# A hybrid decoder step on one core: the second output gate computed between key units, sample products in quarters, the third modulation round spread out

## The chip, the cores and the metric

The kernel runs on one core of one Trainium2 chip, as a single launch. The metric is the device time in microseconds, the median of several runs. Inputs and outputs lie in HBM; everything between them is held in the core's on-chip memory (SBUF, 128 partitions) and in eight accumulator banks (`ps`, PSUM). The engines are TensorE (PE), VectorE (DVE), ScalarE (ACT), GpSimd (POOL) and SyncE (SP), each with its own instruction queue that is worked off in order; they are kept in step by semaphores (`sem(...)`), written out by hand.

## What is computed

One layer for 256 prompt tokens and 8 sample sequences of 4 tokens (288 tokens in all, `T`), model width 1024, all in float32. From the reference, cut:

```python
mod = jnp.dot(jax.nn.silu(c), w_ada) + b_ada             # 6 x 1024 per sequence
sh1, sc1, gt1, sh2, sc2, gt2 = split(mod, 6)
h = rmsnorm(x, g_pre1) * (1.0 + sc1) + sh1
hq, hf, hi, hg, aq, ak, av, ua, ub = split(h @ w_in)     # 4 x 512, 3 x 512, 2 x 1024
# branch a: gated linear recurrence over hq, hf, hi, from state_hgrn for the samples, normed, times silu(hg)
# branch b: attention; samples against 2048 cached keys and values each (16 pages of 128 tokens,
#           found through page_table), of which the best 3 of 8 blocks of 256 and the own tokens count
merged = sigmoid(ua) * (o_a @ w_proj_a) + sigmoid(ub) * (o_b @ w_proj_b)
x = x + gt1 * rmsnorm(merged @ w_out, g_post1)
h = rmsnorm(x, g_pre2) * (1.0 + sc2) + sh2
g_, u_ = split(h @ w_gu)                                 # 2 x 2816
x = x + gt2 * rmsnorm((silu(g_) * u_) @ w_down, g_post2)
```

Outputs are x, the new recurrent states, and the new keys and values.

## The kernel before

**Dense products.** Activations lie transposed, features on partitions, the 288 tokens along the free dimension. A weight tile has 512 input features times 512 columns (1 MB). Since the product is to be as exact as float32, weights and activations are split in a high part and a remainder (`w_hi`, `w_lo`, `h_hi`, `h_lo`), and each product is three matmuls (`three`, lines 1399 to 1401). ScalarE copies a half tile into the high part (L540, and `hi_late`, L555), VectorE subtracts to get the remainder (L897, `lo_late` L906), then TensorE does 24 matmuls of 128x288 for the half tile, 48 for the tile. Tiles 0 to 13 of w_in (`dense_in`) fill `w_hi` and `w_lo`, which have two buffers. Tiles 14 to 21, which give the two output gates `ua` and `ub`, use `wl_hi` and `wl_lo`, with one buffer.

**The ring.** All weights and cached pages go through `ring`, four slots of 1 MB. The list `RING` fixes the order; SyncE issues the loads in this order, and load n waits in `slot_free` until the content of slot n - 4 has been used: a modulation tile (`w_ada`) by its TensorE group (`ada_used`), a w_in tile by the subtraction of its second half (`lo_split`), a key unit by its transpose, a value unit by its matmuls. A key or value unit is four pages of 256 KB.

**Stages.** First the norms and the first modulation round (8 tiles of w_ada); then w_in tiles 0 to 13, with the second round (tiles 8 to 15) in pairs ahead of tiles 0, 2, 3 and 4 and the third (16 to 23) in pairs ahead of tiles 10 to 13. Rotation of q and k, the gate products of the samples (`queries` on GpSimd, L450), the samples' own scores (L1527) and the start of the recurrence lie between them.

Then the *key stage*: 32 key units (`cached_keys`). VectorE transposes a unit into `KT` (two buffers, L1060), TensorE does 32 small matmuls (L1546), and after each four units `restrip` (L1553) rearranges the scores. The list `between` puts other work behind single units: transposes of the recurrence (L1583), and behind units 5, 7, ... 19 the eight `gram` products (L1598) in two sets of banks. Each level of the recurrence goes from GpSimd (`diff`, L464 and L465) to ScalarE (`level_exp`, L647), back to GpSimd (`scale_level`, L475), to TensorE (`gram`), and to VectorE (`keep`, L1084).

Then tiles 14 to 17, while VectorE chooses blocks and ScalarE takes the exponentials; the first value unit (L1565) comes behind tile 17. In the *value stage* (32 units, `values`) the list `after` puts work behind single units: tiles 18 to 21 behind units 1, 3, 5 and 7, the recurrence's output (`hgrn_out`, L1620), the samples' reads of their states (`hgrn_sample_out`, L1627 and L1630: per head 8 matmuls of four columns, with a 128x128 weight load each), `sample_states` (L1639), and from unit 13 the eight heads of the prompt's attention (`prompt_step`: scores, then a mask and a maximum on VectorE from L1223, an exponential on ScalarE L745, normalisation on VectorE, transposes and value products). The four `o_normed` (L1205) and four `sample_state` (L1177, L1184) stand between the first heads on VectorE.

Then the projections, the merge and `w_out`; the *x1 stage* (norm, residual, second norm): channels 0 to 5 of the residual on VectorE (L1312, L1314), channels 6 and 7 on GpSimd (L496, L498), which also does the three operations on the sample tokens (L503 to L508) and all eight `h_lo` of `h_lower(1)` (L436). The feed-forward part follows, and at its end sums over the tokens' features (`token_sums`, L1808) in two groups, in banks 7 and 2, added on VectorE (L1383).

Of the kernel before, what the change touches and what calls it, by code (L numbers as in the profile page):

```python
# [16 lines left out]
F32 = mybir.dt.float32  # L17
# [3 lines left out]
ALU = mybir.AluOpType  # L21
# [35 lines left out]
def constants():  # L57
# [42 lines left out]
    c["seq"] = (p[:, None] // TS == np.arange(NSEQ)[None, :]).astype(float)  # L100
# [15 lines left out]
def build(nc, inp, out):  # L116
# [55 lines left out]
    wl_lo = sb("wl_lo", [P, BK, BC], F32R, "split_area", BK * BC * 4)  # L172
    proj = sb("proj", [P, PT_, T], F32, "proj_area")
# [78 lines left out]
    GROUPS = [4, 5, 6, 1, 0, 2, 3, 7, 8, 9, 10]  # L252
    NF = 7
    NKU = NVU = 4 * NSEQ
    SAMP = slice(TP, T)
    U_BANK = ((4, 7), (5, 0), (6, 1))
    ROOT2 = slice(384, 387)
    ADA_BANK = (4, 6)
    X1_DVE = 6
# [24 lines left out]
    def w_src(name, row, col, rows=BK * P, width=BC):  # L284

        return inp[name][0, bass.ds(row, rows), bass.ds(col, width)].rearrange("(k p) n -> p k n", p=P)

# [18 lines left out]
    with block:  # L306

        @block.sync
        def _(sp):
# [36 lines left out]
            for j in range(4):  # L346
                pages = page_numbers(SPE, 4 * j, 4)
                slot_free(NA + j)
                load_pages(sp, "cache_k", pages, (NA + j) % NSLOT)
            with sp.Fori(1, NSEQ) as b:  # L350
                for j in range(4):
                    pages = page_numbers(SPE, b * NPG + 4 * j, 4)
# [1523 lines left out]
```

## Time and profile before

| | |
|---|---|
| median of 3 runs | 765.85 us (760.8 to 769.72) |
| the profiled execution | 767.38 us, its span 765.5 us |
| mean granted TensorE clock | 0.912 of full speed |
| busy: TensorE, VectorE, ScalarE, GpSimd | 657.4, 413.2, 273.8, 77.2 us |
| HBM traffic | 168.93 MB, mean 221 GB/s |
| DMA busy, tenths in 40 slices of the span | 8895952978999978896565998540464546445201 |
| chain that ended last | PE 66%, DVE 12%, DMA 9%, POOL 4%, SyncE's queue 4%, issue 3%, ACT 2% |

Times inside the kernel are microseconds from the start of the span. The busy time of an engine is the time in which it executes; TensorE's matmuls overlap, so its busy time counts pipelined work. A dense matmul has a mean of 302 ns in the records, but one starts every 131 ns. "Idle before" says what ended an engine's wait. The granted clock is the share of full speed that the chip gave TensorE in a stretch: 1.0 is 2.4 GHz, 0.5 is 1.2 GHz. The DMA share is the mean busy share of the core's 16 DMA engines.

### The profile page before, as it was taken

The numbers are of one execution on the slowest core, as the hardware profiler recorded it, in microseconds if no ns is written. First come the engines' busy times: TensorE is split into PE (matmuls) and PEld (weight loads), VectorE is DVE, ScalarE is ACT, GpSimd is POOL, SyncE is SP. The second block draws the span as 40 slices with busy tenths as digits, with TensorE's granted clock in tenths as the row PEclk, the third lists the DMA queues.
The fourth block names the chain that finished last, engine by engine and source line by source line (L and its number), as shares of the span: only waits on it lengthen the run. The fifth ranks groups of instructions, "written<-read, shape, count | busy, mean of one in ns | idle before, by whom it ended". The sixth has DMA issues, their size and how long they took to land.

```text
span 765.5 us, 13144 instructions
## 1 busy us (share of the span) xinstructions
PE 657.4 (86%) x5251; PEld 552.0 (72%) x5251; DVE 413.2 (54%) x493; ACT 273.8 (36%) x390; POOL 77.2 (10%) x86
## 2 busy tenths in 40 slices
PE   4759999986867769889967759985999999999996
PEld 1237999774655559768423329984999999999996
DVE  0641479357999979320387325767635353543522
ACT  1232435253221136223312223353645454532421
POOL 2040005101364000000000000004200000000001
PEclk9859999997999699997668959998999999999987
DMA  8895952978999978896565998540464546445201
GB/s 334 318 349 209 357 186 87 353 252 290 351 332 307 336 287 230 290 324 203 188 210 157 325 343 274 184 148 0 124 188 153 172 143 190 150 151 182 87 1 62
DMA packets 96305, 168.93 MB, mean 221 GB/s; under 512 B 6449, under 2 KB 37865, under 8 KB 93058
## 3 DMA queue, kind: packets, MB, share of 16 engines
q1 hardware_dynamic: 90386, 162.85, 62.7%
q10 hardware_dynamic: 5152, 3.08, 1.4%
q0 software_dynamic: 720, 2.32, 0.8%
q8 instruction: 35, 0.57, 0.3%
q14 instruction: 12, 0.10, 0.0%
HBM read 163.51 MB, written 4.72 MB: 220 GB/s over the span
## 4 chain that ended last, share of the span: by engine, by line
PE 66%; DVE 12%; DMA 9%; POOL 4%; SPq 4%; issue 3%; ACT 2%; POOLq 0%; DVEq 0%; ACTq 0%
PE ps L1399 17%; PE ps L1401 16%; PE ps L1400 16%; DMA ring<-w_in 6%; DVE KT L1060 4%; SPq L302 2%; DMA ring<-w_ada 2%; PE ps L1565 2%; PE ps L1410 2%; POOL hx L475 2%; PE ps L1598 2%; PE ps L1630 2%; PE ps L1546 2%; PE ps L1762 1%; DVE wl_lo L906 1%
## 5 line engine op out<-in xcount | busy, mean ns | idle before, releaser
L897 DVE TENSOR_TENSOR w_lo<-ring,w_hi 128x1024 fp32r<-128x1024 f32 (+1 forms) x112 | 133.4, 1218 | 124.9 <-ACT w_hi L540 124.8
L1399 PE MATMUL ps<-h_hi,w_hi 128*128 128x288 f32 x576 | 174.1, 302 | 14.4 <-POOL h_lo L436 9.5
L1400 PE MATMUL ps<-h_lo,w_hi 128*128 128x288 f32 x576 | 172.0, 299 | 0.0
L1401 PE MATMUL ps<-h_hi,w_lo 128*128 128x288 f32 x576 | 171.3, 297 | 0.0
L540 ACT ACTIVATE w_hi<-ring 128x1024 fp32r<-128x1024 f32 (+1 forms) x112 | 113.8, 1040 | 153.7 <-PE ps L1401 87.1
L1399 PEld LDWEIGHTS ps<-h_hi,w_hi 128*128 128x128 f32 x576 | 109.9, 191 | 22.5 <-issue 13.1
L1401 PEld LDWEIGHTS ps<-h_hi,w_lo 128*128 128x128 f32 x576 | 110.4, 192 | 0.0
L1400 PEld LDWEIGHTS ps<-h_lo,w_hi 128*128 128x128 f32 x576 | 110.3, 191 | 0.1
L1060 DVE STREAM_TRANSPOSE KT<-ring 128x2048 f32<-128x2048 f32 x32 | 72.3, 2286 | 9.1 <-PE ps L1546 5.7
L1546 PE MATMUL ps<-KT,Wk 128*32 128x128 f32 x1024 | 39.4, 303 | 21.4 <-DVE KT L1060 21.4
L1546 PEld LDWEIGHTS ps<-KT,Wk 128*32 128x32 f32 x1024 | 29.8, 120 | 32.9 <-DVE KT L1060 23.3
L1399 PE MATMUL ps<-f_hi,w_hi 128*128 128x288 f32 x176 | 53.5, 304 | 0.0
L1400 PE MATMUL ps<-f_lo,w_hi 128*128 128x288 f32 x176 | 53.1, 302 | 0.0
L1401 PE MATMUL ps<-f_hi,w_lo 128*128 128x288 f32 x176 | 52.9, 301 | 0.0
L1399 PE MATMUL ps<-h_hi,wl_hi 128*128 128x288 f32 x128 | 38.7, 303 | 9.2 <-DVE wl_lo L906 9.1
L1565 PE MATMUL ps<-ring,Pt 128*32 128x512 f32 x256 | 39.1, 709 | 6.8 <-DMA ring<-cache_v 6.8
L1410 PE MATMUL ps<-ring,cs 128*32 128x512 f32 x192 | 29.3, 723 | 14.5 <-DMA ring<-w_ada 14.5
L1400 PE MATMUL ps<-h_lo,wl_hi 128*128 128x288 f32 x128 | 37.8, 295 | 0.0
L1401 PE MATMUL ps<-h_hi,wl_lo 128*128 128x288 f32 x128 | 37.6, 294 | 0.0
L1401 PEld LDWEIGHTS ps<-f_hi,w_lo 128*128 128x128 f32 x176 | 34.3, 195 | 0.0
L1399 PEld LDWEIGHTS ps<-h_hi,wl_hi 128*128 128x128 f32 x128 | 24.0, 187 | 14.2 <-DVE wl_lo L906 14.2
L1399 PEld LDWEIGHTS ps<-f_hi,w_hi 128*128 128x128 f32 x176 | 34.2, 194 | 0.0
(314 smaller groups left out, 1004.7 us busy)
## 6 DMA issues: line engine op xcount, KB each, us to landing
ring<-cache_k SPq DMA_DIRECT2D x128, 256.0 KB, 4.0
ring<-cache_v SPq DMA_DIRECT2D x128, 256.0 KB, 3.6
ring<-w_ada SPq DMA_DIRECT2D x24, 1024.0 KB, 7.5
ring<-w_in SPq DMA_DIRECT2D x22, 1024.0 KB, 7.8
ring<-w_gu SPq DMA_DIRECT2D x44, 512.0 KB, 4.7
ring<-w_down SPq DMA_DIRECT2D x10, 1024.0 KB, 5.0
ring<-w_out SPq DMA_DIRECT2D x4, 1024.0 KB, 5.4
S<-state_hgrn SPq DMA_DIRECT2D x4, 512.0 KB, 7.3
```

Of the source, the lines that this page charges most:

```text
L302: queue.dma_start(ring[:, s, q * 512:(q + 1) * 512], pools[pool][0, bass.ds(pg, 1), :, :].rearrange("o p n -> p (o n)"))\
L475: ins = pool.tensor_tensor(xv, xv, sv, ALU.mult)
L540: act.activation(w_hi[:, par, k, :], slot4(s)[:, k, :], ACT.Copy).then_inc(sem("hi_split"), 1)
L897: dve.tensor_tensor(w_lo[:, par, k, :], slot4(s)[:, k, :], w_hi[:, par, k, :].bitcast(F32), ALU.subtract).then_inc(sem("lo_split"), 1)
L1060: dve.transpose(KT[:, u % 2, :, :], ring[:, s, :].rearrange("p (g n) -> p g n", n=512)).then_inc(sem("key_slots"), 1)
L1399: pe.matmul(dst, h, x_hi, start=first, stop=False)
L1400: pe.matmul(dst, h, x_lo, start=False, stop=False)
L1401: return pe.matmul(dst, l, x_hi, start=False, stop=last)
L1410: ins = pe.matmul(ps[32 * i:32 * i + 32, ADA_BANK[g % 2], :], cs[:, k, :], ring[:, n % NSLOT, i * BC:(i + 1) * BC], start=k == 0, stop=k = ...
L1546: ins = pe.matmul(ps[32 * a:32 * a + 32, b % 2, j * P:(j + 1) * P], Wk[:, b, m // 2, 2 * a + m % 2, :], KT[:, u % 2, :, c * 32:(c + 1) * 3 ...
L1565: ins = pe.matmul(ps[32 * q:32 * q + 32, g, :], Pt[:, 4 * g + q, i, :], ring[:, n % NSLOT, q * 512:(q + 1) * 512], start=i == 0, stop=False)
L1598: ins = pe.matmul(ps[:, 2 + 2 * (gi % 2) + tt, h * P:(h + 1) * P], left[:, h, tt * P:(tt + 1) * P], right[:, h, tt * P:(tt + 1) * P], star ...
```

## The change

**Input stage.** The third modulation round is no longer loaded in pairs ahead of tiles 10 to 13: one tile comes after each of the tiles 7 to 10, two after 11 and two after 12 (`ADA_AFTER`), in ring and TensorE order alike, and it has a bank of its own. The samples' spread and own scores move together between tiles 8 and 9, the four small operations on `lbt` move ahead on VectorE, and the logarithm and the exponential of the recurrence ahead of `evac_in` on ScalarE. The first key transposes wait only for the dense tiles that used their part of the memory.

**Key stage.** The four tiles of the second output gate `ub` are cut otherwise: `WK`, 1024 input features by 256 columns, each in the ring behind key units 5, 11, 17 and 23. They are worked in eight groups of 24 matmuls (`dense_k`) behind key units 6, 9, ... 27, with new buffers `wk_hi` and `wk_lo` for half a tile, a copy on ScalarE (`hi_k`), the subtraction on GpSimd (`lo_k`) and evacuation by `evac_k`. GpSimd's eight `queries` are spread among its levels. All `gram` results use banks 2 and 3, and `keep` comes one unit earlier.

**Value stage.** Only the four tiles of `ua` (`WL`, 18 to 21) stay behind the keys: three ahead of the values, the last in two halves behind units 1 and 2. The samples' state reads become eight products of 512 columns, four heads side by side in quarters of the array (`sample_reads`), masked on VectorE into `xm`, and added up by eight transposing matmuls. The prompt steps stand behind every second unit from 10 on.

**x1 and the end.** All eight channels of x1 go to VectorE, GpSimd keeps one of three sample operations, the first two `h_lo` go to VectorE. The last token sums are one group in bank 7, read straight by ScalarE.

```diff
-    ADA_BANK = (4, 6)
-    X1_DVE = 6
+    ADA_BANK = (4, 6, 7)
+    LO_DVE = 2
...
-    for w in range(2 * NF):
-        if w in (0, 2, 3, 4) or w >= 10:
-            RING += [("ada", next(a)), ("ada", next(a))]
-        RING.append(("in", w))
+    ADA_AFTER = {-1: 2, 1: 2, 2: 2, 3: 2, 7: 1, 8: 1, 9: 1, 10: 1, 11: 2, 12: 2}
+    for w in range(-1, 2 * NF):
+        if w >= 0:
+            RING.append(("in", w))
+        RING += [("ada", next(a)) for _ in range(ADA_AFTER.get(w, 0))]
     NA = len(RING)
-    RING += [("key", u) for u in range(NKU)]
-    RING += [("in", w) for w in range(14, 18)]
-    for w in range(18, 22):
-        RING += [("value", 2 * (w - 18)), ("value", 2 * (w - 18) + 1), ("in", w)]
-    RING += [("value", v) for v in range(8, NVU)]
+    for u in range(NKU):
+        RING.append(("key", u))
+        if u in (5, 11, 17, 23):
+            RING.append(("in", WK[u // 6]))
+    RING += [("in", w) for w in WL[:3]] + [("value", 0), ("value", 1), ("in", WL[3])]
+    RING += [("value", v) for v in range(2, NVU)]
...
@@ gpsimd @@
+            def lo_k(w, half):
+                pool.wait_ge(sem("hi_split"), w * 2 + (half + 1))
+                pool.tensor_tensor(wk_lo[:, :, :], slot8(N_OF["in", w] % NSLOT)[:, 4 * half:4 * half + 4, :], wk_hi[:, :, :].bitcast(F32), ALU.subtract)\
+                    .then_inc(sem("lo_split"), 1)
...
-            for b in range(NSEQ):
-                queries(b)
+            queries(0)
+            queries(1)
...
-            for li in range(7):
-                scale_level(li)
-                if li + 2 < 7:
-                    diff(li + 2)
+            scale_level(0)
+            queries(2)
+            queries(3)
+            scale_level(1)
+            lo_k(14, 0)
+            lo_k(14, 1)
+            diff(2)
...
+            scale_level(3)
+            lo_k(15, 0)
+            lo_k(15, 1)
+            diff(4)
+            scale_level(4)
+            diff(5)
+            scale_level(5)
+            diff(6)
+            scale_level(6)
+            for w in (16, 17):
+                lo_k(w, 0)
+                lo_k(w, 1)
...
@@ scalar @@
+            def hi_k(w, half):
+                n = N_OF["in", w]
+                if half == 0:
+                    act.wait_ge(sem(f"w_landed{n % NSLOT}"), 16 * in_slot(n))
+                act.wait_ge(sem("w_used"), w * 2 + half)
+                act.activation(wk_hi[:, :, :], slot8(n % NSLOT)[:, 4 * half:4 * half + 4, :], ACT.Copy).then_inc(sem("hi_split"), 1)
...
@@ vector @@
-                if u % 2 == 1 and 7 <= u < 23:
-                    keep((u - 7) // 2)
+                if u % 2 == 0 and 6 <= u < 22:
+                    keep((u - 6) // 2)
...
+            dve.wait_ge(sem("ds_done"), 1)
+            dve.tensor_tensor(xm[:, :, :], ps[:, 2:4, :].rearrange("p t (b e) -> p (t b) e", e=DK), over(C("seq"), 2, DK), ALU.mult).then_inc(sem("vm_ready"), 1)
...
@@ tensor @@
+            def dense_k(w, half):
+                i = w - WK[0]
+                pe.wait_ge(sem("lo_split"), w * 2 + (half + 1))
+                if half == 0:
+                    pe.wait_ge(sem("tile_out"), 4 * NF + 2 * i)
+                for j in range(2):
+                    for kt in range(4):
+                        c = slice(j * P, j * P + P)
+                        ins = three(ps[:, 4 + j, 0:T], (wk_hi[:, kt, c], wk_lo[:, kt, c]), h_hi[:, 4 * half + kt, :], h_lo[:, 4 * half + kt, :],
+                                    half == 0 and kt == 0, half == 1 and kt == 3)
+                    if j == 1:
+                        ins.then_inc(sem("w_used"), 1)
+                    elif half == 1:
+                        ins.then_inc(sem("tile_done"), 1)
...
-            def hgrn_sample_out(h):
+            def sample_reads():
                 pe.wait_ge(sem("s0_landed"), 64)
-                pe.matmul(ps[:, 6, h * TSA:(h + 1) * TSA], hvs[:, h, :], hAs[:, h, :], start=True, stop=False, skip_group_check=True)
+                for g in range(2):
+                    for h in range(HH):
+                        ins = pe.matmul(ps[32 * h:32 * h + 32, 2 + g, :], hqt[:, h, SAMP], S0[:, 4 * g:4 * g + 4, h, :], start=True, stop=True)
+                ins.then_inc(sem("ds_done"), 1)
+
+            def hgrn_sample_out():
+                pe.wait_ge(sem("vm_ready"), 2)
                 for b in range(NSEQ):
-                    c = h * TSA + b * TS
-                    ins = pe.matmul(ps[:, 6, c:c + TS], S0[:, b, h, :], hqt[:, h, TP + b * TS:TP + (b + 1) * TS], start=False, stop=b == NSEQ - 1, skip_group_check=True)
...
+                    pe.matmul(ps[:, 6, 0:P], xm[:, b, :], ident, start=b == 0, stop=False, skip_group_check=True)
+                for h in range(HH):
+                    ins = pe.matmul(ps[:, 6, h * TSA:(h + 1) * TSA], hvs[:, h, :], hAs[:, h, :], start=False, stop=h == HH - 1, skip_group_check=True)
...
+            for i in range(8):
+                between.setdefault(6 + 3 * i, []).append(lambda i=i: dense_k(14 + i // 2, i % 2))
...
-            dense_in(16)
-            dense_in(17)
+            dense_late(20)
...
+            after = {1: [lambda: dense_late(21, (0,))], 2: [lambda: dense_late(21, (1,))], 3: [probs_sum],
+                     4: [hgrn_out, sample_reads], 6: [hgrn_sample_out], 7: [lambda: sample_states(0)], 8: [o_sum], 9: [lambda: sample_states(1)],
+                     11: [lambda: sample_states(2)], 15: [lambda: sample_states(3)], 27: [lambda: sample_out(0)]}
+            for k in range(AH + 2):
+                after.setdefault(10 + 2 * k, []).append(lambda k=k: prompt_step(k))
```

## Rows read from the trace of the kernel before

**Rows 1.** Windows: us, busy us per engine (instructions), granted clock, DMA share, GB/s.

```profile
92.00:172.00 80.00, 75.83 (x603) 68.41 (x602) 51.16 (x58) 32.60 (x44) 14.78 (x22) 0.98 0.63 227
172.00:275.00 103.00, 74.01 (x1241) 56.72 (x1239) 90.61 (x58) 23.93 (x33) 29.96 (x24) 0.87 0.95 327
...
308.00:352.00 44.00, 39.20 (x297) 31.21 (x297) 10.29 (x13) 15.70 (x19) 0.00 (x0) 1.00 0.88 305
352.00:418.00 66.00, 56.08 (x248) 28.25 (x247) 34.97 (x67) 15.39 (x36) 0.00 (x0) 0.69 0.54 172
418.00:449.00 31.00, 20.55 (x144) 8.58 (x147) 8.19 (x27) 5.58 (x20) 0.00 (x0) 0.91 0.96 321
```

**Rows 2.** SyncE's queue and the chain at the end of the values: start, us.

```profile
418.08 25.99 SPq L302 DMA_DIRECT2D ring<-cache_v  x33
...
448.50 1.94 PE ps L1565 x8
```

**Rows 3.** Input stage, 118 to 175: groups, then timelines of VectorE, GpSimd, SyncE.

```profile
L1399 PE MATMUL ps<-h_hi,w_hi 128*128 128x288 f32 x94 | 29.0, 309 | 4.2 <-DVE w_lo L897 4.2
...
L540 ACT ACTIVATE w_hi<-ring 128x1024 fp32r<-128x1024 f32 x8 | 8.1, 1051 | 22.4 <-DMA ring<-w_in 20.9 <-PE ps L1401 1.5
...
120.27 9.75 DVE L1013 TENSOR_TENSOR lbt<-lbt 128x4 f32<-128x4 f32 x1
...
120.58 9.41 POOL L450 TENSOR_TENSOR Wk<-Qrep,const 128x256 f32<-128x256 f32 x16
...
165.59 34.56 SPq L302 DMA_DIRECT2D ring<-cache_k  x43
```

**Rows 4.** Windows of the feed-forward part and of the value stage.

```profile
560.00:580.00 20.00, 20.00 (x152) 20.00 (x151) 11.06 (x11) 12.08 (x13) 0.00 (x0) 1.00 0.48 146
...
360.00:380.00 20.00, 20.00 (x72) 9.92 (x72) 5.83 (x8) 4.33 (x7) 0.00 (x0) 0.54 0.43 136
```

**Rows 5.** Groups of the key stage, and the page's DMA issues: KB, us to landing.

```profile
L1060 DVE STREAM_TRANSPOSE KT<-ring 128x2048 f32<-128x2048 f32 x32 | 72.3, 2286 | 9.1 <-PE ps L1546 5.7 <-PE ps L1401 3.4
L1546 PE MATMUL ps<-KT,Wk 128*32 128x128 f32 x1024 | 39.4, 303 | 21.4 <-DVE KT L1060 21.4
...
L475 POOL TENSOR_TENSOR hx<-hx,proj 128x512 f32<-128x512 f32 (+1 forms) x14 | 19.1, 1390 | 24.7 <-ACT hx L647 24.7
...
L1553 PE MATMUL ps<-raw,const 128*128 128x512 f32 x14 | 8.8, 714 | 0.0
...
ring<-cache_k SPq DMA_DIRECT2D x128, 256.0 KB, 4.0
```

**Rows 6.** From keys to values: ScalarE's timeline, then the chain of waits.

```profile
274.77 0.60 ACT L637 ACTIVATE raw<-ps 128x512 f32<-128x512 f32 x1 [4.73 <-PE ps L1546]
...
299.67 0.62 DVE Pt L1137
...
308.11 1.04 PE ps L1565 x8
```

**Rows 7.** Value stage: one group, then VectorE's timeline at heads 0 and 3.

```profile
L1630 PE MATMUL ps<-hqt,S 128*128 128x4 f32 x64 | 12.7, 330 | 0.0
...
384.62 0.27 DVE L1223 TENSOR_TENSOR pa<-ps,const 128x128 f32<-128x128 f32 x1
...
408.37 0.28 DVE L1223 TENSOR_TENSOR pa<-ps,const 128x128 f32<-128x128 f32 x1
```

**Rows 8.** The x1 stage: timelines of VectorE, ScalarE and TensorE.

```profile
517.25 1.05 DVE L1312 TENSOR_TENSOR proj<-proj,rs 128x288 f32<-128x288 f32 x1
...
521.11 0.45 DVE L1312 TENSOR_TENSOR proj<-proj,rs 128x288 f32<-128x288 f32 x1
...
527.14 0.50 ACT L816 ACTIVATE rs<-ps,const 128x288 f32<-128x288 f32 x1 [2.23 <-PE ps L1762]
...
534.20 0.37 PE L1399 MATMUL ps<-h_hi,w_hi 128*128 128x288 f32 x1 [3.07 <-POOL h_lo L436]
```

**Rows 9.** The end of the kernel: VectorE's timeline.

```profile
758.64 0.16 DVE L1383 TENSOR_TENSOR stat<-stat,ps 128x2 f32<-128x2 f32 x1 [3.20 <-PE ps L1808]
```

More of the change, by code:

```diff
@@ L172, in build @@
     wl_lo = sb("wl_lo", [P, BK, BC], F32R, "split_area", BK * BC * 4)
+    wk_hi = sb("wk_hi", [P, 4, 256], F32R, "split_area", 24576)
+    wk_lo = sb("wk_lo", [P, 4, 256], F32R, "split_area", 28672)
     proj = sb("proj", [P, PT_, T], F32, "proj_area")
@@ L345, in _ @@
             sp.wait_ge(sem("table_ready"), 1)
[L346 to L352, printed above, removed]
-                    sp.wait_ge(sem("key_slots"), b * 4 + (j - 3))
-                    load_pages(sp, "cache_k", pages, (NA + j) % NSLOT)
-            for n in range(NA + NKU, N_OF["value", 16]):
+            for n in range(NA, N_OF["value", 16]):
                 kind, i = RING[n]
@@ L432, in h_lower @@
             def h_lower(time):
-                for k in range(DT):
+                for k in range(LO_DVE if time else 0, DT):
                     pool.wait_ge(sem("h_hi"), time * DT + k + 1)
+                    if time and k == LO_DVE:
+                        pool.wait_ge(sem("h_lo"), DT + LO_DVE)
                     pool.tensor_tensor(h_lo[:, k, :], h32[:, k, :], h_hi[:, k, :].bitcast(F32), ALU.subtract).then_inc(sem("h_lo"), 1)
@@ L980, in _ @@
             lo_a(6)
+            dve.wait_ge(sem("lb_exp"), 1)
+            link(dve.tensor_tensor(lbt[:, 3, :], lbt[:, 1, :], lbt[:, 2, :], ALU.add))
+            link(dve.reciprocal(lbt[:, 3, :], lbt[:, 3, :]))
+            link(dve.tensor_tensor(lbt[:, 4, :], lbt[:, 1, :], lbt[:, 3, :], ALU.mult))
+            link(dve.tensor_scalar(lbt[:, 5, :], lbt[:, 4, :], -1.0, 1.0, ALU.mult, ALU.add))
             lo_a(7)
@@ L1144, in _ @@
             choose(1)
-            lo_late(15, 1)
+            lo_late(19, 1)
             dve.wait_ge(sem("max_spread"), 1)
@@ L1321, in _ @@
                     t.append(mark(dve.tensor_tensor(h32[:, k + 1, 0:TP], xT[:, k + 1, 0:TP], rs[:, 0:TP], ALU.mult)))
+                if k == 0:
+                    need(at_r)
+                    dve.tensor_tensor(h_samp, h_samp, over(modT[:, 24:32, 1:CC], 3, TS), ALU.add).then_inc(sem("h_samples"), 1)
                 need(t[k])
                 dve.tensor_scalar(h32[:, k, 0:TP], h32[:, k, 0:TP], gain[:, k, 0:1], modT[:, 24 + k, 0:1], ALU.mult, ALU.add).then_inc(sem("h_ready"), 1)
-                if k == 3:
+                if 1 <= k <= LO_DVE:
+                    dve.wait_ge(sem("h_hi"), DT + k)
+                    dve.tensor_tensor(h_lo[:, k - 1, :], h32[:, k - 1, :], h_hi[:, k - 1, :].bitcast(F32), ALU.subtract).then_inc(sem("h_lo"), 1)
+                if k == 5:
                     lo_b(31)
@@ L1597, in gram @@
                     for h in range(HH):
-                        ins = pe.matmul(ps[:, 2 + 2 * (gi % 2) + tt, h * P:(h + 1) * P], left[:, h, tt * P:(tt + 1) * P], right[:, h, tt * P:(tt + 1) * P], start=True, stop=True)
+                        ins = pe.matmul(ps[:, 2 + tt, h * P:(h + 1) * P], left[:, h, tt * P:(tt + 1) * P], right[:, h, tt * P:(tt + 1) * P], start=True, stop=True)
                 if gi == 0 or LEVELS[li] <= 2:
```

329 lines of the change are left out of this document (167 added, 162 removed).

## The prediction

> **What bounds the kernel now.** I read the stages first, then who ends the waits in each, then SyncE's queue. The profiled execution took 767.4 us around a span of 765.5, 1.5 us above the median of the three runs (765.85); the sum goes against 767.4. [rows 1] show two kinds of stage ahead of the feed-forward part. While cached keys are read (172 to 275) the DMA is busy 0.95 of the time at 327 GB/s and VectorE 90.6 of 103 us: both go at the pace of one key unit (1 MB, 32 of them) per 3.2 us, TensorE being busy 74 us. From 308 to 449 the value units and four w_in tiles take 141 us, though 36 MB at the pace of the stage's end need only 113: between 352 and 418 the DMA is busy 0.54. Only from 418 to 449 is it DMA-bound again (0.96), with 33 page loads in 25.99 us, 3.15 us for a unit of four [rows 2]. So the middle of the kernel is one stream of 73 MB through a ring of four slots, and what counts is how long it stands still: key unit 1 is issued at 165.6 [rows 3], the last value unit used at 448.5 [rows 2], 283 us for 230 us of transfer.
>
> **Input stage.** TensorE waits 4.2 us for split weights, and behind that ScalarE 20.9 us for w_in to land [rows 3]. Two causes: the third modulation round is loaded in pairs ahead of tiles 10 to 13, after idle DMA time; and a 128x4 operation of VectorE stands for 9.75 us, as long as GpSimd's sixteen products (9.41), so the split of tile 10, its slot and the next loads come late [rows 3]. The change puts the loads after tiles 7 to 12 and the 128x4 operations ahead of that time; only two of eight product groups remain there. The round costs TensorE the same groups, merely earlier, and its loads meet a DMA that is 0.37 idle [rows 1]. I take the 4.2 us as gone: the last dense tile ends at 168.6 instead of 172.8, and key unit 1, which waits for a modulation slot in both kernels, is issued at 161.4. Bounds: 0 and twice that, since the first transposes may also start earlier.
>
> **Key stage.** Added here: four w_in loads, eight TensorE groups of 24 matmuls, eight ScalarE copies, eight GpSimd subtractions, eight evacuations. 152 such matmuls take 20 us at full clock [rows 4], so a group 3.15 us and all 25; on 74 busy of 103 that would fit. Transfer: the new tiles come in rows of 1 KB instead of 2. The w_gu stretch, all 1 KB rows, moves 146 GB/s at a share of 0.48, 304 at full share [rows 4]; the values 321 at 0.96, 334 [rows 1]. So a tile takes 3.45 us, four 13.8. The Trainium skill, DMA: Bandwidth & Descriptors, section Specifications, has transfers of 512 B and more at line rate; by that four tiles would take 12.6 and the sum fall by 1.2 us. The rows decide.
>
> The larger cost is a wait. wk_hi and wk_lo have one buffer: the second half of a tile can't be split until the first group has run, and the slot of the tile, which the third key unit after it needs, is held until GpSimd has done that second subtraction. The first group stands behind key unit 6 (12, 18, 24), and what follows is serial: transpose 2.29, 32 key products 1.23, at units 12 and 24 a restrip of 1.26 (8.8 us for seven) [rows 5], group 3.15, ScalarE copy 1.05 [rows 3], subtraction of 1024 on GpSimd, issue to landing 4.0 [rows 5]. GpSimd's price at this size isn't in the trace: 256 elements take 0.59 in the products [rows 3], so 2.35; 512 take 1.39 in the scaling [rows 5], so 2.8 above; I take 2.35, the longer run of like instructions. From the landing of unit 6 to that of unit 9 it is 14.1 us (15.3 with the restrip), where the stream needs 3 x 3.15 = 9.4: gaps of 4.6 and 5.9, two each, 21.0. SyncE stands at this wait, so the loads of units 10 and 11 are late too. At unit 18 the first subtraction also stands behind the last level's exponential and scaling, an estimate of 1.5 from those rows: 22.5. Bounds of a gap: 0, if the ring runs ahead, and 10, if a level of the recurrence comes between each time. GpSimd's 19 us more fit in 130; VectorE keeps its 32 transposes and gains slack.
>
> End of the stage: unit 1 lands at 165.4, 30 units at 3.2 make it 261.4, tiles and gaps 297.7; transpose, products and the last block sums 4.9, and 1.0 for gram results that have one buffer instead of two: 303.6. Now the last key products end at 274.7 [rows 6]: 29 us later.
>
> **Softmax stage.** VectorE's chain is the same. But value unit 0 started at 308.1, behind a fourth tile, while the probabilities and the third tile were there at 300.3 [rows 6]; now three tiles stand ahead. With 0.1 for the handover it starts 25.7 instead of 33.4 us after the keys: 329.3.
>
> **Value stage.** Units 0, 1, the last tile and unit 2 are in the ring by then; unit 3 waits for unit 0's slot and lands at 329.3 + 1.1 + 4.0 = 334.4, and 28 more at 3.15 end at 422.6. TensorE must not stop this stream. It was busy 39.2 + 56.1 + 20.6 = 116 us [rows 1]; three tiles go (20), the 64 records of four-column products with the state (12.7 [rows 7]) and their companions (2) become 8 products of 512 columns and 12 small ones, an estimate of 4 from the value units' 1.04 per four [rows 6]. About 85 are left. The prompt heads go every second unit, 6.3 us. Three steps took 23.75 us while states and norms stand between [rows 7], 7.9 each, so VectorE falls behind by 1.6 us three times, and the ring absorbs only part: I add 4. The last unit is used at 426.6 instead of 448.5, 22 us earlier. From there to x1 nothing changes.
>
> **x1 and the end.** Two of eight channels leave GpSimd. While it worked, a VectorE operation took 1.05 instead of 0.45 [rows 8]. Sixteen at a start-to-start of 0.37 from 516.9 end at 522.8, the last square at 523.3, the root comes at 524.4 instead of 527.1 if TensorE's sums keep up. VectorE takes two sample operations, but GpSimd's chain goes, and the first two h_lo come from VectorE: TensorE starts at 531.5 instead of 534.2 [rows 8], 2.7 us. Bounds 0 and 4. At the end VectorE's addition of partial sums ahead of the square root goes [rows 9], one root and one reciprocal come: 0.3 gained, between -0.5 and 0.8.
>
> **Sum:** 767.4 - 22 - 2.7 - 0.3 = 742.4. Set to the median it is 741; I stay at 742. The input gain is inside the 22.
>
> **Rivals.**
> *No gap.* The waits in the key stage are hidden: 22.5 us less, 720. For it: VectorE transposes two units ahead. Against: the serial sum has no parallel part. Chance 0.12.
> *Clock.* The value stage becomes TensorE-bound. From 352 to 418 the granted clock is 0.69 [rows 1], so 0.62 of the time at 1.2 GHz, the rest at 2.4; of the 41 us left of its work that is 13 us of stretching, and 85 is 72 at full clock. With a share f at 1.2 GHz the stage takes 72 x (1 + f); it binds from f = 0.35 (97 us). At 0.55 it is 112 and the time 757: chance 0.17. From f = 0.78 (128 us) the kernel is slower than before by over 1%; with all of it at 1.2 GHz it is 144 and 789: chance 0.07. For it: 360 to 380, with no idle time on TensorE and a grant of 0.54 [rows 4]. Against: that stretch is mostly the narrow products that are removed. The Trainium skill, TensorE: Matmul & The Clock Gate, section What's actually happening, has activity release the throttle; by it a busier TensorE would be at 2.4 GHz and this rival at nothing, but the stretch from 360 to 380 speaks against it.
> *Long gaps.* The split queues cross with the recurrence's and a gap is 10: 18 us more, 760. For it: GpSimd has 19.1 us of scaling in this stage [rows 5], and a half tile that waits for TensorE now stands ahead of a difference. Chance 0.12.
> *The forecast* as summed, 733 to 752: 0.52.
>
> **Numbers.** About 1% (7.7 us) is what a measurement tells from no change. Faster by over 1% (below 758.2): forecast, no gap, most of the first clock case, 0.80; within 1%: the long gaps and the rest, 0.12; slower 0.08. The range leaves out half of the no-gap case and the slow clock case: 726 to 760.
>
> **What would show it.** Some 130 us from first to last key products, with four stretches of idle DMA of 5 us in which SyncE waits for GpSimd's wk_lo; value unit 0 some 26 us after the keys, the values even at 3.15 us to the end; no 9.75 us operation; tile 13 done near 169; h_lo first from VectorE. Wrong, if TensorE's idle time in the key stage is released by the recurrence, if the DMA share after 335 is below 0.85, or if TensorE in the value stage shows a clock near 0.6 and no idle time.

## The result, and the profile after

The changed kernel takes 757.7 us (median of 4 runs, 755.27 to 759.93) against 767.8 (760.8 to 771.1) for the kernel before on the same chip: a ratio of 0.990, with a 95% interval of 0.986 to 0.994. All ratios here are taken over executions in the fast state alone and are not quotients of the medians (here 0.987). It is faster, by 1.0%; forecast was 742, 3.1%. The profiled execution took 758.5 us around a span of 756.7, 8.8 less than the span of before.

First the windows of the changed kernel: the key stage, its four stretches of idle DMA, then the value stage. They answer to [rows 1].

```profile
core 0: us, PE busy (x) PEld busy (x) DVE busy (x) ACT busy (x) POOL busy (x), PEclk, DMA share, GB/s
168.00:319.00 151.00, 105.45 (x1447) 88.55 (x1445) 90.17 (x57) 35.88 (x50) 55.79 (x44) 0.85 0.74 257
188.00:200.00 12.00, 11.54 (x168) 10.22 (x161) 9.59 (x8) 2.68 (x4) 4.87 (x3) 0.93 0.36 129
219.00:231.00 12.00, 11.58 (x162) 9.69 (x154) 9.49 (x7) 3.20 (x4) 7.31 (x5) 1.00 0.29 104
249.00:266.00 17.00, 13.80 (x202) 12.18 (x200) 10.16 (x8) 4.23 (x5) 7.97 (x4) 0.90 0.22 73
283.00:296.00 13.00, 8.97 (x136) 7.43 (x135) 8.09 (x5) 3.32 (x5) 4.70 (x2) 1.00 0.45 165
345.00:444.00 99.00, 84.44 (x508) 37.76 (x504) 51.80 (x109) 29.86 (x67) 0.00 (x0) 0.87 0.95 322
```

The shape of the forecast is there: four gaps in the key stage, and values that come at 0.95 of the DMA from end to end. But the gaps are deep. One minus the DMA share, times the length, is 7.7, 8.5, 13.3 and 7.1 us of idle DMA, 36.6 in all (an estimate that takes a share of 1 as full); 22.5 were forecast.

Two groups of the page, which answer to [rows 5], and its DMA issues:

```profile
L1116 DVE STREAM_TRANSPOSE KT<-ring 128x2048 f32<-128x2048 f32 x32 | 73.5, 2302 | 44.9 <-DMA ring<-cache_k 38.5
L1623 PE MATMUL ps<-KT,Wk 128*32 128x128 f32 x1024 | 39.3, 302 | 41.4 <-DVE KT L1116 41.4
...
ring<-cache_k SPq DMA_DIRECT2D x128, 256.0 KB, 4.5
```

The transposes cost what they did, but VectorE now sat idle for 38.5 us until a page of keys landed, where before it waited 9.1 us and for TensorE. Behind it TensorE waited 41.4 instead of 21.4.

The first gap, engine by engine. Timelines of SyncE's queue (start, duration), ScalarE, GpSimd and VectorE:

```profile
178.16 9.89 SPq L313 DMA_DIRECT2D ring<-cache_k  x12
...
199.93 7.44 SPq L313 DMA_DIRECT2D ring<-cache_k  x12
...
187.48 0.60 ACT L689 ACTIVATE S<-ps 128x512 f32<-128x512 f32 x1 [7.02 <-PE ps L1630]
187.98 1.05 ACT L590 ACTIVATE wk_hi<-ring 128x1024 fp32r<-128x1024 f32 x1
196.28 1.06 ACT L590 ACTIVATE wk_hi<-ring 128x1024 fp32r<-128x1024 f32 x1 [7.25 <-PE ps L1458]
...
189.10 2.36 POOL L495 TENSOR_TENSOR wk_lo<-ring,wk_hi 128x1024 fp32r<-128x1024 f32 x1 [5.62 <-ACT wk_hi L590]
197.41 2.36 POOL L495 TENSOR_TENSOR wk_lo<-ring,wk_hi 128x1024 fp32r<-128x1024 f32 x1 [5.95 <-ACT wk_hi L590]
...
189.41 2.31 DVE L1116 STREAM_TRANSPOSE KT<-ring 128x2048 f32<-128x2048 f32 x1 [3.41 <-DMA ring<-cache_k]
...
206.28 2.31 DVE L1116 STREAM_TRANSPOSE KT<-ring 128x2048 f32<-128x2048 f32 x1 [5.15 <-DMA ring<-cache_k]
```

Unit 6 has landed at 189.4. TensorE's group for the first half runs from 192.78 to 196.23, behind that unit's products; ScalarE copies the second half right behind it, GpSimd subtracts until 199.77, SyncE issues unit 9 at 199.93, having stood still since 188.05. Each link is near its forecast (the group 3.45 for 3.15). What isn't is the last: the unit is there at 206.28, 6.35 us after its first issue. Page by page, its four loads are issued at 199.93, 200.45, 201.71 and 202.22 and land 2.9, 3.5, 2.9 and 4.0 us later: a page doesn't take longer than the 4.0 forecast, but the fourth is issued 2.3 us after the first.

The third gap has more causes. GpSimd, ScalarE and TensorE:

```profile
251.30 3.31 POOL L487 TENSOR_TENSOR hx<-hx,proj 128x576 f32<-128x576 f32 x2 [4.87 <-ACT hx L694]
254.57 2.35 POOL L495 TENSOR_TENSOR wk_lo<-ring,wk_hi 128x1024 fp32r<-128x1024 f32 x1
263.12 2.35 POOL L495 TENSOR_TENSOR wk_lo<-ring,wk_hi 128x1024 fp32r<-128x1024 f32 x1 [6.20 <-ACT wk_hi L590]
...
261.98 1.06 ACT L590 ACTIVATE wk_hi<-ring 128x1024 fp32r<-128x1024 f32 x1 [9.81 <-PE ps L1458]
...
256.97 0.40 PE L1456 MATMUL ps<-h_hi,wk_hi 128*128 128x288 f32 x1 [3.20 <-POOL wk_lo L495]
```

The split copied at 251.1 is subtracted only after the last level's scaling, so TensorE waits 3.20 us; and its group, from 256.97 to 261.94, takes 4.97 us, part of it at 1.2 GHz. The gram products behind unit 17 also stand ahead of unit 18's own products: these start at 252.7, 3.6 us after the unit has landed at 249.1, where a transpose of 2.3 was counted.

The x1 stage, where [rows 8] showed operations of 1.05 us: VectorE's two reciprocals and TensorE's first feed-forward product.

```profile
510.40 1.95 DVE L1361 RECIPROCAL rs<-rs 128x288 f32<-128x288 f32 x1 [1.25 <-ACT rs L861]
...
520.46 1.95 DVE L1370 RECIPROCAL rs<-rs 128x288 f32<-128x288 f32 x1 [2.09 <-ACT rs L867]
...
526.40 0.37 PE L1456 MATMUL ps<-h_hi,w_hi 128*128 128x288 f32 x1 [2.50 <-DVE h_lo L1386]
```

From the first reciprocal to the product it is 16.0 us; before, 514.88 to 534.20, it was 19.3.

Where the time stands at each mark, in the profiled executions (starts and ends of these instructions on TensorE, us):

| | before | after | forecast |
|---|---|---|---|
| last dense tile of the input stage | 172.8 | 170.7 | 168.6 |
| last key products end | 274.7 | 318.5 | 303.6 |
| value unit 0 | 308.0 | 344.8 | 329.3 |
| last value unit | 448.5 | 443.9 | 426.6 |
| first feed-forward product | 534.2 | 526.4 | 509.5 |
| span | 765.5 | 756.7 | 740.5 |

### The profile page after: what moved, and what is told of

Read it like the earlier page. It is cut to its first block, busy times and chain, and to the rows that moved or that the text cites. A ratio compares the mean times of both kernels' runs of the same rounds, so it can differ in the third digit from the quotient of the medians.

```text
span 756.7 us, 13015 instructions
## 1 busy us (share of the span) xinstructions
PE 650.0 (86%) x5219; PEld 545.0 (72%) x5219; DVE 396.1 (52%) x490; ACT 274.3 (36%) x391; POOL 88.1 (12%) x86
## 4 chain that ended last, share of the span: by engine, by line
PE 63%; DMA 11%; SPq 8%; DVE 8%; issue 3%; POOL 3%; ACT 3%; POOLq 0%; DVEq 0%; ACTq 0%
PE ps L1456 17%; PE ps L1457 16%; PE ps L1458 16%; SPq L313 6%; DMA ring<-cache_k 4%; DMA ring<-w_in 4%; DVE KT L1116 2%; SPq L307 2%; DMA ring<-w_ada 2%; PE ps L1623 2%; POOL wk_lo L495 2%; PE ps L1467 2%; DMA ring<-cache_v 1%; PE ps L1847 1%; PE ps L1676 1%
## 5 line engine op out<-in xcount | busy, mean ns | idle before, releaser
L1116 DVE STREAM_TRANSPOSE KT<-ring 128x2048 f32<-128x2048 f32 x32 | 73.5, 2302 | 44.9 <-DMA ring<-cache_k 38.5
L1623 PE MATMUL ps<-KT,Wk 128*32 128x128 f32 x1024 | 39.3, 302 | 41.4 <-DVE KT L1116 41.4
L1457 PEld LDWEIGHTS ps<-f_lo,w_hi 128*128 128x128 f32 x176 | 34.2, 194 | 0.0
L1395 DVE TENSOR_TENSOR fu<-ps,fa 128x576 f32<-128x576 f32 x11 | 8.3, 757 | 44.1 <-PE ps L1458 24.5
L541 POOL TENSOR_TENSOR x1c<-yc,x1c 32x512 f32<-32x512 f32 x2 | 2.5, 1256 | 215.9 <-ACT yc L932 215.9
L1642 PEld LDWEIGHTS ps<-ring,Pt 128*32 128x32 f32 x256 | 6.3, 118 | 28.6 <-DMA ring<-cache_v 19.8
```

The costliest lines, as they stand in the source:

```text
L1116: dve.transpose(KT[:, u % 2, :, :], ring[:, s, :].rearrange("p (g n) -> p g n", n=512)).then_inc(sem("key_slots"), 1)
L1457: pe.matmul(dst, h, x_lo, start=False, stop=False)
L1623: ins = pe.matmul(ps[32 * a:32 * a + 32, b % 2, j * P:(j + 1) * P], Wk[:, b, m // 2, 2 * a + m % 2, :], KT[:, u % 2, :, c * 32:(c + 1) * 3 ...
L1642: ins = pe.matmul(ps[32 * q:32 * q + 32, g, :], Pt[:, 4 * g + q, i, :], ring[:, n % NSLOT, q * 512:(q + 1) * 512], start=i == 0, stop=False)
```

## Experiments

The kernels of each group of runs shared a chip, and each ratio is against the kernel before on that chip. Stage times are from each kernel's profiled execution. A difference from the changed kernel's time is one of medians taken on different chips, where the kernel before had 764.9 to 767.8 us; by the ratios it would come out up to 3 us otherwise. A kernel called "the changed kernel with ..." differs from it by what is shown alone.

**A tile in two halves.** If the slot is held because the second half can't be split before the first group has run, a half with a slot of its own must free the ring, with all work and all orders kept.

```diff
-        if u in (5, 11, 17, 23):
-            RING.append(("in", WK[u // 6]))
+        if u % 3 == 2 and 5 <= u <= 26:
+            RING.append(("ink", (u - 5) // 3))
...
-                act.activation(wk_hi[:, :, :], slot8(n % NSLOT)[:, 4 * half:4 * half + 4, :], ACT.Copy).then_inc(sem("hi_split"), 1)
+                act.activation(wk_hi[:, :, :], slot8(n % NSLOT), ACT.Copy).then_inc(sem("hi_split"), 1)
```

> Each w_in tile of the key stage is loaded as two halves, each in a slot of its own behind key units 5, 8, 11, ..., 26; same matmuls, copies and subtractions in the same order. Theory (a slot is held through the first group of TensorE because wk_hi and wk_lo have one buffer): a slot now goes free 4 to 7 us after its half lands, less than three key units take (9.4), so the four stretches of idle DMA (36.6 us in all, by the windows of the changed kernel) shrink to under 8; last key products near 290 instead of 318.5; time 26 to 32 us below the changed kernel, about 729. Rival A (TensorE is the bound: 11.5 of 12 us busy in the first two gaps, part of it at 1.2 GHz): the idle DMA time stays above 20 us, now behind VectorE or key_slots, gain at most 12, time about 746. Rival B (the transfers in rows of 1 KB are what costs): gain 0.

Measured: 734.8 us, ratio 0.9625 (0.956 to 0.969), 23 us below the changed kernel; last key products end at 293.5, 25 earlier. Windows of the key stage, of where its first gap was, of two remaining gaps, and of the value stage; then GpSimd, and ScalarE:

```profile
168.00:293.50 125.50, 101.54 (x1444) 85.31 (x1442) 89.41 (x57) 35.20 (x49) 55.82 (x44) 0.89 0.88 309
190.00:195.00 5.00, 5.00 (x74) 4.44 (x66) 4.96 (x4) 1.10 (x2) 0.00 (x0) 1.00 0.73 262
210.00:215.00 5.00, 2.76 (x40) 1.61 (x40) 4.56 (x4) 1.92 (x3) 4.79 (x3) 1.00 0.37 127
235.00:250.00 15.00, 11.80 (x152) 10.09 (x151) 11.29 (x8) 3.25 (x5) 9.27 (x6) 0.89 0.40 133
320.00:422.40 102.40, 84.70 (x504) 37.85 (x496) 51.74 (x109) 29.77 (x67) 0.00 (x0) 0.87 0.93 309
...
212.44 2.36 POOL L496 TENSOR_TENSOR wk_lo<-ring,wk_hi 128x1024 fp32r<-128x1024 f32 x1
...
210.28 1.05 ACT L590 ACTIVATE wk_hi<-ring 128x1024 fp32r<-128x1024 f32 x1
```

The same TensorE work (105.5 us in the stage of the changed kernel, 101.5 now) fits in a stage 25 us shorter, so it was not the bound, and the transfers, of the same rows, weren't either. The theory holds, though its size was too large: 15 us of idle DMA are left (0.12 of 125.5), mostly at 210 to 215 and 235 to 250. There SyncE stands for 5.6 and 7.0 us before the load of a half tile, whose slot is that of the half before, until GpSimd has subtracted (at 214.80 the first time). GpSimd's scaling of the recurrence makes that subtraction 1.1 and 2.4 us late, but more is lost ahead of it, on ScalarE: TensorE was through with `wk_hi` at about 206.6, and the copy came at 210.28, behind an evacuation, the recurrence's exponential (which itself waited 1.72 us for GpSimd) and a copy of scores; 3.7 us the first time, about as much the second. The value stage is 3.6 us longer than in the changed kernel, so not all of the 25 arrives.

**The subtraction on VectorE.** The eight `lo_k` leave GpSimd:

```diff
             for u in range(NKU):
                 turn_keys(u)
+                if u % 6 == 0 and 6 <= u <= 24:
+                    lo_k(13 + u // 6, 0)
+                if u % 6 == 2 and 8 <= u <= 26:
+                    lo_k(13 + u // 6, 1)
```

> The eight wk_lo subtractions go from GpSimd (2.36 us) to VectorE, each behind the transpose of key unit 6, 8, 12, 14, ... Theory (serial chain): VectorE takes 1.22 for 1024 elements, so 1.1 less in each chain, 4.5 in four, and the 3.2 us that TensorE waited for GpSimd at the third tile go too: 7 us faster than the changed kernel, about 751; gaps of SyncE 12, 11, 16, 13 us become about 11, 10, 11, 12. Rival (VectorE's queue is late with it, since the subtraction stands behind a transpose that waits for its page): gain under 2.

Measured: 756.0 us, ratio 0.990 (0.983 to 0.997), no different from the changed kernel. Yet its last key products end at 309.9, 8.6 earlier: the theory's gain is there in the main, and lost again. 1.4 of the 8.6 were there before the stage (last dense tile at 169.4). The four stops of SyncE are 13.3, 9.5, 12.6 and 13.4 us where the changed kernel has 11.9, 11.1, 15.9 and 12.7: the third is shorter as expected, the first and the fourth are longer, which stays unexplained; from the landing of the unit ahead of each stop to that of the unit behind it, all four take 69.8 us instead of 74.5. Value unit 0 comes 28.4 us after them (26.3 in the changed kernel), and the value stage takes 104.6 instead of 99.1. Its windows there:

```profile
338.00:443.00 105.00, 85.52 (x511) 38.35 (x513) 52.41 (x110) 29.98 (x67) 0.00 (x0) 0.87 0.89 303
378.00:386.00 8.00, 3.39 (x15) 1.58 (x15) 6.79 (x13) 1.36 (x5) 0.00 (x0) 0.70 0.96 333
386.00:402.00 16.00, 16.00 (x56) 5.83 (x59) 9.03 (x19) 2.36 (x10) 0.00 (x0) 0.51 0.68 233
```

TensorE first waits (busy 3.39 of 8 us, VectorE 6.79), then works 16 us without a pause at a grant of 0.51, which is 1.2 GHz nearly throughout, and the DMA falls to 0.68: here, as the order suggests, TensorE holds the slots.

**The groups one unit earlier.**

```diff
-                between.setdefault(6 + 3 * i, []).append(lambda i=i: dense_k(14 + i // 2, i % 2))
+                between.setdefault(5 + 3 * i, []).insert(0, lambda i=i: dense_k(14 + i // 2, i % 2))
```

> Each of the eight groups of TensorE one key unit earlier (behind units 5, 8, 11, ... and ahead of the gram products there), nothing else. Theory: the first group of a tile starts when its split is done, near the landing of the next key unit, not 3.4 us behind that landing; chain 3 us shorter per gap, 8 to 13 us faster than the changed kernel in all, about 748. Rival (TensorE now waits for the tile with key products queued behind it, and the transposes behind those): gain under 3.

Measured: 766.4 us, ratio 1.003 (0.999 to 1.008): 9 us slower than the changed kernel, which neither side expected. GpSimd at the second tile, and ScalarE behind it:

```profile
219.86 2.35 POOL L495 TENSOR_TENSOR wk_lo<-ring,wk_hi 128x1024 fp32r<-128x1024 f32 x1
232.55 2.37 POOL L495 TENSOR_TENSOR wk_lo<-ring,wk_hi 128x1024 fp32r<-128x1024 f32 x1 [10.35 <-ACT wk_hi L590]
...
230.94 0.60 ACT L689 ACTIVATE S<-ps 128x512 f32<-128x512 f32 x1 [11.60 <-PE ps L1630]
231.43 1.05 ACT L590 ACTIVATE wk_hi<-ring 128x1024 fp32r<-128x1024 f32 x1
```

TensorE waited 4.53 us for this split, with key products behind it. It was through with the group at 227.04, but ScalarE's copy of the second half came 4.4 us later: in ScalarE's order the scores of a sample stand ahead of it, and TensorE's restrip, on which these wait, now comes after the group. At the fourth tile it is the same (group through at about 294.6, copy at 299.61). SyncE's stops are 10.2, 16.5, 13.3 and 17.0 us: at the first and third tile, where no restrip stands there, they are 1.7 and 2.7 us shorter than in the changed kernel, as the theory has it, at the second and fourth 5.3 and 4.2 longer. One engine's order was moved, the other's wasn't.

**Few matmuls.** 18 of the 24 matmuls of each group are left out (`for kt in range(1)`).

> Leaves out 18 of the 24 matmuls of each of the eight groups; loads, splits, waits and evacuations stay. Theory (the group is one link of 3.5 us of a serial chain of some 15): links of 0.9, so 2.6 less in each of four gaps, 3.6 in the third (half clock there): 10 to 12 us faster than the changed kernel, about 746. Rival A (the work of TensorE as a whole, 25 us and the clock, is what makes the stage long): 20 to 25 us faster, about 735. If it gives nothing the group is not in the chain.

Measured: 743.9 us, ratio 0.975 (0.966 to 0.983), 13.8 below the changed kernel, and key products that end 15.0 earlier, at 303.5. That is near the theory and short of rival A: of TensorE's work what counts is the link in the chain. The four stops of SyncE fell from 11.9, 11.1, 15.9 and 12.7 us to 9.5, 9.6, 9.5 and 10.6, 12.4 us in all.

**Both.** Half tiles, and the subtraction on VectorE behind units 6, 9, ..., 27.

> Half tiles (as in the run with half tiles, 734.8) and the wk_lo subtractions on VectorE behind the transposes of units 6, 9, ..., 27. Theory: what is left of idle DMA with half tiles (17.6 us from 165 on, most of it at 209 to 250) stands behind GpSimd's scaling of the recurrence, in whose queue wk_lo waits (a split copied at 211.3 is subtracted at 212.4 to 214.8, one copied at 241.1 at 243.5 to 245.8); off that queue 6 to 9 us go in the key stage, last key products near 286. In the end 0 to 9 of it: in the run with lo on VectorE alone 8.6 us won in the key stage were down to 1.1 at the last value unit, with a granted clock of 0.50 there; likeliest 729. Rival: VectorE has no slack left at 3.2 us per unit, gain 0 in the key stage.

Measured: 728.2 us (727.39 to 733.04), ratio 0.950 (0.944 to 0.956), the best version together with the one built on it below, 29.5 us faster than the changed kernel. The profiled execution is the slowest of its five, 733.0. Its last key products end at 290.8, 2.7 earlier than with half tiles alone, less than the 7 or so expected; the stage began 1.6 us later (last dense tile 171.9 against 170.3), and ScalarE's order, which holds up the copy, is as it was. Windows of the key stage and the value stage, then three stretches of the latter:

```profile
172.00:290.80 118.80, 95.33 (x1426) 79.15 (x1424) 99.59 (x65) 34.09 (x46) 40.05 (x36) 0.94 0.91 315
317.50:420.00 102.50, 84.87 (x505) 37.55 (x504) 52.12 (x109) 29.98 (x67) 0.00 (x0) 0.86 0.90 309
356.00:364.00 8.00, 3.35 (x23) 1.07 (x22) 6.81 (x14) 1.36 (x5) 0.00 (x0) 0.81 1.01 364
364.00:372.00 8.00, 8.00 (x29) 2.96 (x28) 6.74 (x14) 1.36 (x5) 0.00 (x0) 0.50 0.88 304
372.00:380.00 8.00, 8.00 (x33) 3.07 (x35) 3.72 (x8) 0.00 (x0) 0.00 (x0) 0.62 0.52 167
```

VectorE is now at 99.6 of 118.8 us in the key stage. In the value stage the same pattern stands as above: TensorE waits for VectorE, then it runs at half clock, and then the DMA is at 0.52.

**The narrow products back.** The changed kernel with `hgrn_sample_out(h)` of before behind value units 4, 5, 5 and 6, and `xm` gone.

> The changed kernel with the 128 products of four columns with the state back in place of the 8 of 512 columns and their 12 followers, behind value units 4 to 6. They cost TensorE 10.7 us more (12.7 + 2 - 4). Theory (the value stage is bound by the DMA, TensorE busy 85 of 99 us): the ring takes up part, 2 to 6 us slower than the changed kernel, about 762. Rival A (TensorE and its clock bind there): 10 or more slower. Rival B: all hidden, within 1.

Measured: 773.0 us, ratio 1.011 (1.002 to 1.020), 15 slower than the changed kernel: rival A. Three windows of its value stage:

```profile
340.00:360.00 20.00, 20.00 (x153) 14.64 (x153) 7.47 (x14) 10.23 (x13) 0.00 (x0) 0.97 0.91 307
360.00:384.00 24.00, 24.00 (x86) 13.23 (x87) 5.83 (x8) 4.77 (x7) 0.00 (x0) 0.53 0.60 201
384.00:457.00 73.00, 54.83 (x304) 21.39 (x307) 37.42 (x86) 14.96 (x48) 0.00 (x0) 0.84 0.87 289
```

For 24 us TensorE is busy without a pause at a grant of 0.53, and 9.6 us of DMA are lost; from value unit 0 to the last it is 116.3 us instead of 99.1. The products of four columns run from 355.1 to 371.4; the low clock sets in while they run and ends at about 383, over 10 us after the last of them. So the rewritten products are worth some 15 us, and all other parts of the change together, the moved tiles among them, cost some 7 (773.0 against 765.5 on that chip, with an interval from 1 to 15): without the rewritten products the change would have made the kernel slower.

**The modulation round in pairs again.**

```diff
-    ADA_AFTER = {-1: 2, 1: 2, 2: 2, 3: 2, 7: 1, 8: 1, 9: 1, 10: 1, 11: 2, 12: 2}
+    ADA_AFTER = {-1: 2, 1: 2, 2: 2, 3: 2, 9: 2, 10: 2, 11: 2, 12: 2}
```

> The changed kernel with the third modulation round loaded in pairs behind w_in tiles 9 to 12 again, as in the kernel before; the 128x4 operations keep their new places. Theory (the pairs were a cause of the late loads): last dense tile and key unit 1 later by 2 to 4 us, and the kernel by as much, about 760. Rival (the 9.75 us operation alone was the cause): within 1.

Measured: 764.4 us (756.34 to 766.12), ratio 0.995 (0.991 to 1.000); the interval touches that of the changed kernel. In the trace the last dense tile ends at 175.6 instead of 170.7, 4.9 later, and is followed by key products 3.3 later at the end of the stage; the rest of the profiled execution's 7.4 is a value stage of 104.5 us. The nine kernels with the loads spread end their last dense tile between 166.8 and 171.9, so 175.6 lies outside their range. The spread seems worth a few microseconds (4 by the ratios, 7 by the medians), from the loads and not only from the long operation; the times alone don't separate the two kernels.

**x1 on VectorE alone, in the kernel before.** One constant, `X1_DVE = 8` for 6.

> The kernel before with all eight channels of x1 on VectorE, the sample operations still on GpSimd. Theory: no operation of 1.05 us there, the second reciprocal 2.7 us earlier, TensorE's first feed-forward product at about 531.5 instead of 534.2, the kernel 2.7 us faster than before. Rival: eight channels on one engine take as long, 0.

Measured: 762.9 us, ratio 0.996 (0.9916 to 0.9995), as forecast. All sixteen operations of the channels take 0.45 or 0.46 us, with none on GpSimd beside them; before, the first four took 1.04 or 1.05. VectorE's two reciprocals and TensorE's first product:

```profile
514.07 1.95 DVE L1307 RECIPROCAL rs<-rs 128x288 f32<-128x288 f32 x1 [1.25 <-ACT rs L807]
524.71 1.95 DVE L1316 RECIPROCAL rs<-rs 128x288 f32<-128x288 f32 x1 [2.66 <-ACT rs L816]
...
531.22 0.37 PE L1399 MATMUL ps<-h_hi,w_hi 128*128 128x288 f32 x1 [3.07 <-POOL h_lo L436]
```

17.2 us from the first to the product instead of 19.3: 2.2 of the 3.3 gained in that stage come from the channels, the rest, by difference, from the sample operations and the first `h_lo`.

**The states spread, and vms on GpSimd.** Two attempts at the value stage, each on top of the best version. In the first:

```diff
-                     11: [lambda: sample_states(2)], 15: [lambda: sample_states(3)], 27: [lambda: sample_out(0)]}
+                     13: [lambda: sample_states(2)], 19: [lambda: sample_states(3)], 27: [lambda: sample_out(0)]}
...
-                if h in (1, 3):
-                    sample_state(2 + h // 2)
+                if h in (2, 5):
+                    sample_state(2 + h // 5)
```

> On top of half tiles with wk_lo on VectorE (728.2): TensorE's state products of heads 2 and 3 behind value units 13 and 19 instead of 11 and 15, and VectorE's updates of these states before prompt heads 2 and 5 instead of 1 and 3. Theory (value stage): from some 40 us after value unit 0 VectorE is busy 6.8 of 8 us, TensorE waits for its masks (busy 3.35 of 8 at 356), the granted clock then falls to 0.50 and for 10 us the ring stands still (DMA 0.52 at 372); with 3.6 us of VectorE's work out of that stretch the wait of TensorE shrinks and the value stage goes from 102.5 to 98 us: 3 to 5 us faster, about 724. Rival (the clock falls there whatever VectorE does, or falls elsewhere): within 1.5.

> On top of half tiles with wk_lo on VectorE (728.2): the three products vms of 32x1024 (1.20 us each) go from VectorE to GpSimd, which has nothing to do in the value stage. Theory: as with the spread states, VectorE has 3.6 us less in the crowded stretch, 2 to 4 us faster, about 725. Rival (as in x1, where a VectorE operation took 1.05 instead of 0.45 us while GpSimd worked): VectorE's operations beside it get slower by as much, within 1.5, or slower.

Measured: 727.0 us (726.86 to 728.53), ratio 0.949 (0.945 to 0.953), with the states spread; 732.8, ratio 0.955 (0.949 to 0.960), with vms on GpSimd. The value stage with the states spread, and three stretches at the place of those above:

```profile
315.50:413.40 97.90, 82.74 (x509) 37.28 (x511) 51.99 (x109) 29.96 (x67) 0.00 (x0) 0.90 0.96 321
354.00:362.00 8.00, 8.00 (x44) 3.80 (x40) 4.91 (x12) 1.36 (x5) 0.00 (x0) 0.90 0.99 350
362.00:370.00 8.00, 4.32 (x32) 1.51 (x31) 6.84 (x13) 1.36 (x5) 0.00 (x0) 0.95 0.99 327
370.00:378.00 8.00, 8.00 (x38) 3.46 (x36) 6.74 (x17) 1.63 (x6) 0.00 (x0) 0.62 0.93 307
```

The stage is 97.9 us long, 4.6 less than in the profiled execution without it, and the DMA doesn't fall below 0.93 there. In the medians that is 1.2 us, within the rival's bound: four of the five runs without it, at 727.4 to 728.4, had presumably lost little to start with. What it may take away is the execution in which the ring stands still; four runs are too few to show it. vms on GpSimd isn't better: on the same chip as the spread states its runs lie 5.7 us higher in the median, and why wasn't followed up.

## Why the prediction was wrong in size

The time, 757.7 us, lies above the 733 to 752 that had a chance of 0.52.

**Input stage:** 2.1 us gained instead of 4.2 (last dense tile 170.7), within the bounds given. Kernels with the same input stage end it between 166.8 and 171.9, so the 2.1 is within their spread; undoing the spread loads alone cost 4.9.

**Key stage, the step that failed.** The mechanism was right: one buffer, the second split behind the first group, the slot behind GpSimd. The term for the waits, 22.5 us, was mis-sized: 36.6. The prices of its links were right or nearly so: GpSimd's 1024 elements 2.36 us (2.35 forecast), a group 3.45 at 2.4 GHz (3.15), the copy 1.06. Two were not. "Issue to landing 4.0" was the time of one page, while a unit is four pages issued one after another: in the four gaps the unit was there 6.35, 5.32, 6.36 and 5.21 us after its first issue, 5.8 in the mean, and 7.2 us more in all. The page itself was priced rightly, the fourth one landing 3.0 to 4.0 us after its own issue; left out were the 1.6 to 3.3 us from the first issue to the fourth. In a full ring this is hidden; after a stop nothing hides it. This is read from the trace, and no run tests it by itself. And the third gap, allowed 6.1 (4.6 for a chain without restrip, 1.5 for the level), lost 13.3: beside the landing the wait for GpSimd was 1.7 longer than allowed, and the group, part of it at half clock, 1.8 longer than the 3.15 counted. These make 10.7 of the 14.1 missing; the gram products ahead of unit 18's (1.3) and groups of 3.45 to 3.75 in the other gaps where I had 3.15 make most of the rest. The chain as a whole bears this out: from the landing of units 6, 12, 18 and 24 to that of the third unit behind each it took 16.9, 18.1, 22.9 and 16.7 us, where the forecast had 14.1, 15.3, 15.6 and 15.3: some 14 us more in all.

My "long gaps" rival had the direction, with 10 us a gap and 760 us, from queues that cross in every gap, and it named what happened in the third gap alone; that its time came within 2 us of the median is luck, since three of the four gaps were long for another reason. Half tiles confirm the cause, few matmuls the link. Of the three signs of being wrong that the prediction named none appeared; the idle time was simply longer than allowed: 147 us from the first to the last key products where 130 were named.

The transfer of the tiles was not the matter. The windows of the changed kernel with a tile in them ran at shares of 0.96 and 0.99 with 323 and 340 GB/s (200 to 219, 231 to 249), too alike to tell my 3.45 us a tile from the 3.15 of equal rates. The rule of the Trainium skill that I set against the rows (DMA: Bandwidth & Descriptors, Specifications) would have moved the sum by 1.2 us, and no run here settles it.

**Softmax stage:** 26.3 us from keys to values, 25.7 forecast.

**Value stage:** 99.1 us to the start of the last unit, 97.3 forecast, DMA at 0.95. That was right for the profiled execution, and not safe: with the DMA as the bound TensorE has only some 15 us of slack, and across the kernels without narrow products the stage took from 97.9 to 104.6. The clock rival is no separate case but this spread, worth up to 6 us. In the changed kernel the clock fell too (0.51 from 383.3 to 391.3, TensorE busy all the time), but the DMA stayed busy in that stretch and little was lost. Why the narrow products mattered I had half right: as work of TensorE, 10.7 us more, they would have hidden in that slack; brought back, they cost 15 us in the medians and 17 in the stage. The Trainium skill (TensorE: Matmul & The Clock Gate, What's actually happening) has activity release the throttle; the trace doesn't agree in the stretch where the narrow products run, 24.00 of 24 us busy at a grant of 0.53, and it agrees in so far as the other low stretches looked at come after a wait of TensorE.

**x1 and end:** 3.3 and 1.0 us gained, 2.7 and 0.3 forecast.

The sum by steps, measured less forecast: input 2.1, gaps 14.1, the rest of the key stage -1.3, softmax 0.6, value stage 1.8, from there to the first reciprocal 0.1, x1 and end -1.3: 16.1, which is the 16 us between 742.4 and 758.5.

## What to carry to other kernels

Work put into a stream through a ring is priced by how long it holds its slot, with every engine that the release passes through, not by its busy time: with the same eight groups put in, the last key products end 44 us later than before with whole tiles, and 16 to 19 with half tiles. When a wait stops a stream, price the restart by all issues of the first unit: the pages of the first unit behind each stop took 2.5 to 4.1 us each, the unit of four 5.2 to 6.4. And follow the gain to the next bound stage: 8.6 us won in the key stage were 1.1 at the last value unit.

## What the runs showed of the hardware

At the same place in the same value stage, 38.5 to 46.5 us after value unit 0, TensorE is busy only 2.9 to 3.5 of 8 us, with waits for VectorE and for values, in six kernels: half tiles, the subtraction on VectorE, the groups early, few matmuls, both, and the pairs. In all six 1.2 GHz follows. In four of them the next 8 us stand at a grant of 0.50 with TensorE busy all the time, and the DMA falls to 0.52 to 0.60 in the 8 us behind; with the groups early and with few matmuls the next 8 us stand at 0.71, and the loss is smaller. Then it is 2.4 GHz again. How long the low clock lasts differs between kernels in which TensorE does much the same there: 17 us in the profiled execution of "both", 24 with the pairs; why is open. At 1.2 GHz the eight records of a value unit take 1.94 us instead of 1.06, so 8 us of it hold work that takes some 4 at 2.4 GHz, an estimate from these records: a wait of some 4 us can cost TensorE as much again behind it. That the wait brings the low clock about is what the order suggests; the run with the states spread (TensorE busy 4.32 of 8, then a grant of 0.62 for 8 us) speaks for it without proving it. Unexpected too: with the products of four columns TensorE was busy throughout and yet at 1.2 GHz for over 20 us, the last 11 of them behind these products.
